# The sample's four RWKV steps on DVE, one operation at a time between the blocks' work, instead of on POOL beside it

## The chip, the cores and the metric

The kernel runs on one NeuronCore of a Trainium2 chip. The metric is the device time of one execution in microseconds (us). Before the change it is 5521.59 us, the median of three runs (5516.73 to 5526.84). The engines are TensorE (PE; PEld is its weight load), VectorE (DVE), ScalarE (ACT), GpSimd (POOL) and SyncE (SP), which here only issues DMAs.

## The reference

It is one inference step of a two-layer decoder trunk, for one prompt of 1024 tokens and for eight samples of four tokens each. The change touches layer 1's RWKV-7 mixing of the samples. Its state S has 64x64 numbers for each of 8 samples x 8 heads, and each of the four tokens takes it one step on:

```python
def step(s, inp):
    r_t, w_t, k_t, v_t, kk_t, a_t = inp
    s_kk = jnp.einsum('bhvk,bhk->bhv', s, kk_t)
    s = (s * w_t[:, :, None, :] - s_kk[..., None] * (kk_t * a_t)[:, :, None, :]
         + v_t[..., None] * k_t[:, :, None, :]).astype(s.dtype)
    return s, jnp.einsum('bhvk,bhk->bhv', s, r_t)
```

The prompt's 1024 tokens go through the same recurrence, but in a chunked form made of matrix products. Layer 1 also has a sparse attention, which needs for every query the 256 largest of its index scores; this kernel finds the 256th largest by a bitwise search.

## The kernel before

The program is a row of stages. The stage of the change is `rwkv_chunks` (L2785, tiles named `rwc_`), from 3215 to 3888 us of the span. Three pieces of work share it:

1. **The prompt's recurrence**, on PE, ACT and DVE: eight blocks of 128 tokens (the loop over `t`, numbered 0 to 7 here), each of two chunks of 64. In a block, DVE masks eight products from PSUM (`rwc_pr`, L3050), makes `rwc_NL` and `rwc_Y` (L3057 to L3061), then adds into `rwc_Y` twelve times (L3070) while PE and ACT square a triangular matrix, six rounds of two. Then come `rwc_RT` (L3076), two `rwc_ZN` (L3080), for each chunk two `rwc_Ms` and one `rwc_M` (L3089, L3094), and the block's output `rwc_y` (L3099). PE starts the next block's transposes only when `rwc_y` is done (`y_ready`), and its two steps of the state (L2995) wait for `rwc_ZN` and `rwc_M`.
2. **The search** (`key_search`, L2353; its generator `rounds`, L2386), on DVE alone. It goes over seven rows of scores (384 to 1028 wide), 32 bits, four pieces a bit, and then three pieces a row to write out the selection: 149 pieces. A piece ends at a `yield`.
3. **The sample's steps** (`rwkv_steps`, L2712, its `steps` L2750), on POOL alone: 128 partitions (sample, head, half of the values), each with 32x64 = 2048 numbers of `S` in `rwc_s_S`. A step is seven operations of 2048 elements and two sums over the keys, each sum a tree of six additions.

DVE's program sets the order by hand: `pick_round` (L3040) runs one piece of the search and stands at fixed places ("slots") of a block: after `rwc_pr` 4 and 8, after the second `rwc_Y` copy, after each of the rounds j = 1 to 5 of the `rwc_Y` additions, five more in a row behind the last of them (`for _ in range(5)`, L3073), after `rwc_RT`, after each `rwc_ZN`, after each `rwc_M`, and after `rwc_y`. That is 2+1+5+5+1+2+2+1 = 19 a block, 152 in all. What is left of the search runs behind the last block (L3102).

A `Chain` (`link`) gives each operation of the search and of the steps a semaphore that the engine itself waits for before the next one. SP issues the loads of the samples' state and vectors in block 1's place, and behind block 7 in this order: the block's `rwc_y`, seven rows of the selection (L2381), the samples' state and outputs (L2743, L2747, behind the semaphore `ready`), and the prompt's state (L2878). The next stage, `rwkv_output` (tiles `rwo_`), begins when all engines have ended this one.

Of the kernel before, what the change touches and what calls it, by code (L numbers as in the profile page):

```python
# [2 lines left out]

# [4 lines left out]
ALU = mybir.AluOpType  # L8
ACT = mybir.ActivationFunctionType
AX_X = mybir.AxisListType.X  # L10
# [768 lines left out]
def wide(ap, shape):  # L779

    return ap.broadcast_to(shape)
# [1653 lines left out]
CH = 64  # L2435

W_A, W_NB, W_K, W_R, W_V, W_LW, W_G, W_BONUS = range(8)
# [274 lines left out]
def rwkv_steps(nc, ph, A, rw, y_out, state_out):  # L2712


    VH = CH // 2
    BH = DEC_BATCH * HEADS
    S = ph.sb("s_S", [P, VH, CH])
    vec = ph.sb("s_vec", [P, DEC_SEQ, 6, CH])
    v2 = ph.sb("s_v2", [P, DEC_SEQ, VH])
    u = ph.sb("s_u", [P, VH])  # L2720
    y = ph.sb("s_y", [P, DEC_SEQ, VH])
    t1 = ph.sb("s_t1", [P, VH, CH])
    ld = ph.sem("s_ld")
    own = ph.sem("s_own")
    ready = ph.sem("s_ready")
    st = ph.sem("s_st")
    n_ld = 16 * (2 + 2 * DEC_SEQ * DEC_BATCH)

    def loads(sp):
        for x in range(2):  # L2730
            rows = slice(x * BH, (x + 1) * BH)
            sp.dma_start(S[rows, :, :].rearrange("p v k -> p (v k)"),
                         A["state_rwkv"][0].rearrange("b h (x v) k -> x (b h) (v k)", x=2)[x]).then_inc(ld, 16)
            for b in range(DEC_BATCH):
                for t in range(DEC_SEQ):
                    src = rw[SEQ + b * DEC_SEQ + t, 0:6, :].rearrange("a (h d) -> h a d", h=HEADS)
                    sp.dma_start(vec[x * BH + b * HEADS:x * BH + (b + 1) * HEADS, t, :, :], src).then_inc(ld, 16)

    def stores(sp):
        sp.wait_ge(ready, 1)  # L2740
        for x in range(2):
            rows = slice(x * BH, (x + 1) * BH)
            sp.dma_start(state_out.rearrange("b h (x v) k -> x (b h) (v k)", x=2)[x],  # L2743
                         S[rows, :, :].rearrange("p v k -> p (v k)")).then_inc(st, 16)
            for b in range(DEC_BATCH):
                dst = y_out[SEQ + b * DEC_SEQ:SEQ + (b + 1) * DEC_SEQ, :].rearrange("t (h x v) -> x h t v", h=HEADS, x=2)[x]
                sp.dma_start(dst, y[x * BH + b * HEADS:x * BH + (b + 1) * HEADS, :, :]).then_inc(st, 16)  # L2747
        sp.wait_ge(st, 16 * 2 * (1 + DEC_BATCH))

    def steps(pool):  # L2750
        link = Chain(pool, own)
        tt = nc.gpsimd.tensor_tensor
        shape = [P, VH, CH]

        def sum_keys(out):

            n = CH // 2
            while n > 1:
                link(tt(t1[:, :, 0:n], t1[:, :, 0:n], t1[:, :, n:2 * n], ALU.add))
                n //= 2  # L2760
            return tt(out.unsqueeze(2), t1[:, :, 0:1], t1[:, :, 1:2], ALU.add)

        pool.wait_ge(ld, n_ld)
        for x in range(2):
            rows = slice(x * BH, (x + 1) * BH)
            link(nc.gpsimd.tensor_copy(v2[rows, :, :], vec[rows, :, W_V, x * VH:(x + 1) * VH]))
        for t in range(DEC_SEQ):
            key = lambda a: wide(vec[:, t, a, :].unsqueeze(1), shape)
            link(tt(t1[:, :, :], S[:, :, :], key(W_A), ALU.mult))
            link(sum_keys(u[:, :]))  # L2770
            link(tt(S[:, :, :], S[:, :, :], key(W_LW), ALU.mult))
            link(tt(t1[:, :, :], wide(u[:, :].unsqueeze(2), shape), key(W_NB), ALU.mult))
            link(tt(S[:, :, :], S[:, :, :], t1[:, :, :], ALU.add))
            link(tt(t1[:, :, :], wide(v2[:, t, :].unsqueeze(2), shape), key(W_K), ALU.mult))
            link(tt(S[:, :, :], S[:, :, :], t1[:, :, :], ALU.add))
            link(tt(t1[:, :, :], S[:, :, :], key(W_R), ALU.mult))
            last = sum_keys(y[:, t, :])
            if t + 1 < DEC_SEQ:
                link(last)
        last.then_inc(ready, 1)  # L2780

    return loads, steps, stores


def rwkv_chunks(nc, A, rw, y_out, state_out, sample_state_out, scores, scores_sample, sel, sel_sample):  # L2785
# [7 lines left out]
    with Phase(nc, "rwc") as ph:  # L2793
# [50 lines left out]
        block = ph.block()  # L2844
# [5 lines left out]
        def _(sp):  # L2850
# [27 lines left out]
                sp.dma_start(state_out.rearrange("(i g) v k -> g v i k", g=2)[g], mt[:, :, g * CH:(g + 1) * CH]  # L2878
                             ).then_inc(end_st, 16)
            sp.wait_ge(end_st, 32)  # L2880

        @block.gpsimd
        def _(pool):
            sample_steps(pool)

        def sq_count(j, g):

# [147 lines left out]
        @block.vector  # L3035
        def _(dve):
            tt = nc.vector.tensor_tensor
            search = rounds(dve)

            def pick_round(dve):  # L3040
                next(search, None)

            dve.wait_ge(const_ld, n_const)
            nc.vector.memset(M[:, :, :], 0.0).then_inc(m_ready, 1)
            own = 0
            for t in range(PT):
                s = t % 2
                for h in range(HEADS):
                    dve.wait_ge(prod_mm, HEADS * t + h + 1)
                    tt(pr[:, h].rearrange("p a c -> p (a c)"), ps[:, 4 + h % 4, :],  # L3050
                       masks[:, 0:4, :].rearrange("p a c -> p (a c)"), ALU.mult).then_inc(prod_ev, 1)
                    if h % 4 == 3:
                        pick_round(dve)
                low = NL[:, 0, 1].rearrange("p (i g) c -> p g i c", g=2)
                for g in range(2):
                    dve.wait_ge(low_mm, 2 * t + g + 1)
                    tt(low[:, g], ps[:, g, :].rearrange("p (i c) -> p i c", c=P),  # L3057
                       wide(masks[:, 4, :].unsqueeze(1), [P, HP, P]), ALU.mult).then_inc(low_ev, 1)
                nc.vector.tensor_copy(Y[:, :, 0, :], x[:, s, X_A, :].rearrange("p (h d) -> p h d", h=HEADS)).then_inc(y_set, 1)
                dve.wait_ge(akv_mm, t + 1)  # L3060
                nc.vector.tensor_copy(Y[:, :, 1, :], ps[:, 2, :].rearrange("p (h d) -> p h d", h=HEADS)).then_inc(y_set, 1)  # L3061
                pick_round(dve)
                dve.wait_ge(y_set, 2 * (t + 1))
                for j in range(POW):
                    for g in range(2):
                        n = 2 * POW * t + 2 * j + g
                        dve.wait_ge(app_mm, n + 1)
                        yg = Y[:, 4 * g:4 * g + 4].rearrange("p h a c -> p (h a c)")
                        at_least(dve, app_ev, n - 1)
                        tt(yg, ps[:, 4 + g, :], yg, ALU.add).then_inc(app_ev, 1)  # L3070
                    if j:
                        pick_round(dve)
                for _ in range(5):  # L3073
                    pick_round(dve)
                dve.wait_ge(r_mm, t + 1)
                tt(RT[:, :, :], ps[:, 6, :].rearrange("p (i c) -> p i c", c=P), xT[:, :, 1, :], ALU.add).then_inc(r_ev, 1)  # L3076
                pick_round(dve)
                for c in range(2):
                    dve.wait_ge(zn_mm, 2 * t + c + 1)
                    tt(ZN[:, c, 0], ps[:, 4 + c, 0:HP * CH].rearrange("p (i k) -> p i k", k=CH),  # L3080
                       wide(eye2[:, :].unsqueeze(1), [P, HP, CH]), ALU.add).then_inc(z_ev, 1)
                    pick_round(dve)
                dve.wait_ge(pc_ev, t + 1)
                for c in range(2):
                    dve.wait_ge(step_mm, 2 * t + c + 1)
                    dve.wait_ge(zn_ev, 2 * t + c + 1)
                    for g in range(2):
                        rows = slice(64 * g, 64 * g + 64)
                        last = tt(Ms[rows, :, :], ps[rows, 2 + g, 0:HP * CH].rearrange("p (i k) -> p i k", k=CH),  # L3089
                                  ZN[rows, c, 1], ALU.add)  # L3090
                    last.then_inc(m_own, 1)
                    own += 1
                    dve.wait_ge(m_own, own)
                    tt(M[:, :, :], Ms[:, :, :], wide(pcs[:, :, c:c + 1], [P, HP, CH]), ALU.mult).then_inc(m_ready, 1)  # L3094
                    pick_round(dve)
                dve.wait_ge(y0_ev, t + 1)
                for g in range(2):
                    yv = y0[:, s, :].rearrange("p (i g v) -> p g i v", g=2, v=CH)[:, g]
                    last = tt(yv, ps[:, g, 0:HP * CH].rearrange("p (i v) -> p i v", v=CH), yv, ALU.add)  # L3099
                last.then_inc(y_ready, 1)  # L3100
                pick_round(dve)
            for _ in search:  # L3102
                pass
# [276 lines left out]
```

## Time and profile before

| | us |
|---|---|
| median of three runs | 5521.59 |
| profiled execution, its own time | 5522.32 |
| its span, first to last instruction | 5520.7 |
| DVE busy in the span | 2389.5 |
| POOL busy in the span | 979.5 |
| POOL in the samples' steps | from 3258.2 to 3427.2 |
| end of `rwc_y` of blocks 0 to 7 | 3312.2, 3419.1, 3492.9, 3568.1, 3643.1, 3717.6, 3791.8, 3867.6 |
| first instruction of the next stage on DVE | 3888.3 |

The profile is of one execution; a timeline row gives start, duration, engine, line, operation, tiles, and in brackets the idle time before it and what ended it. A row of a group gives the count behind an x, then the busy time in us, the mean of one in ns, and the idle time before. A row of windows gives the length of the stretch, then for PE, PEld, DVE, ACT and POOL the busy time and the instructions, then PE's granted clock as a share of full speed, the share of the DMA engines and their rate.

### The profile page before, as it was taken

Reading aid. Unit: us, or ns where it says so; the run is one execution under the profiler, and the core shown is the slowest. Engines: PE = TensorE matmul, PEld = TensorE weight load, DVE = VectorE, ACT = ScalarE, POOL = GpSimd, SP = SyncE. Lnnn points to the kernel's source line nnn. Section 1 sums busy time; section 2 is a strip of 40 time slices with the busy share of each in tenths; the row PEclk is TensorE's granted clock in tenths of the full one; section 3 lists DMA queues with packets and bytes.
Section 4 is the critical chain, followed back from the end, with each engine's and each line's share of the span. In section 5 each row is a group of like instructions: output and inputs, shape, how many; then the busy total and the mean of one; then the engine's idle time right before and its main releaser. Section 6 shows DMA issues by size and latency. Waiting matters only on the chain. (4 is left out here: it accounts for less than half of the span.)

```text
span 5520.7 us, 56273 instructions
## 1 busy us (share of the span) xinstructions
PE 4248.7 (77%) x21425; PEld 3301.4 (60%) x21425; DVE 2389.5 (43%) x3646; ACT 1101.7 (20%) x2150; POOL 979.5 (18%) x569
## 2 busy tenths in 40 slices
PE   7756749778799978799707866787176876999799
PEld 6534534336799956577603245677054445999667
DVE  3067640212555521210036567777596133655410
ACT  1123220110111122111014421121153201111121
POOL 2000000000122223222022338000001110222133
PEclk9855656889799989899755567878588987999899
DMA  3211010453211122222133320000413532111220
GB/s 126 72 26 23 12 30 8 134 172 88 63 46 46 38 64 70 78 98 75 51 122 104 111 77 27 28 28 3 131 37 95 159 119 76 50 46 46 64 67 31
DMA packets 239659, 377.87 MB, mean 68 GB/s; under 512 B 106923, under 2 KB 113852, under 8 KB 238079
## 3 DMA queue, kind: packets, MB, share of 16 engines
q1 hardware_dynamic: 213462, 285.77, 17.0%
q0 software_dynamic: 26000, 89.51, 5.3%
q8 instruction: 121, 1.98, 0.1%
q14 instruction: 76, 0.62, 0.0%
HBM read 292.93 MB, written 88.98 MB: 69 GB/s over the span
## 5 line engine op out<-in xcount | busy, mean ns | idle before, releaser
L91 PE MATMUL ffn_up_hp<-ffn_up_xT,ffn_up_w_high 128*128 128x352 f32 x4224 | 1017.1, 324 | 9.5 <-DVE ffn_up_xT L198 9.5
L91 PEld LDWEIGHTS ffn_up_hp<-ffn_up_xT,ffn_up_w_high 128*128 128x128 f32 x4224 | 737.5, 190 | 11.4 <-DVE ffn_up_xT L198 11.4
L91 PE MATMUL ffn_up_hp<-ffn_up_xT,ffn_up_w_low 128*128 128x352 f32 x2112 | 680.7, 322 | 0.0
L91 PEld LDWEIGHTS ffn_up_hp<-ffn_up_xT,ffn_up_w_low 128*128 128x128 f32 x2112 | 399.7, 189 | 0.0
L91 PE MATMUL ffn_down_acc<-ffn_down_w_high,ffn_down_a_high 128*128 128x512 f32 (+1 forms) x792 | 324.5, 410 | 84.3 <-DVE ffn_down_w_low L752 55.1
L91 PE MATMUL od_in_acc<-od_in_w_high,od_in_xT 128*128 128x512 f32 (+3 forms) x1152 | 353.7, 388 | 1.0 <-POOL od_in_w_low L273 1.0
L474 POOL TENSOR_TENSOR ffn_up_w_low<-ffn_up_w,ffn_up_w_high 128x1024 fp32r<-128x1024 f32 x88 | 211.3, 2401 | 760.3 <-DVE ffn_up_w_high L84 760.3
L91 PE MATMUL ffn_down_acc<-ffn_down_w_low,ffn_down_a_high 128*128 128x512 f32 (+1 forms) x792 | 319.5, 403 | 0.0
L91 PE MATMUL ffn_down_acc<-ffn_down_w_high,ffn_down_a_low 128*128 128x512 f32 (+1 forms) x792 | 318.2, 402 | 0.0
L728 POOL TENSOR_TENSOR ffn_down_a_low<-ffn_act_actT,ffn_down_a_high 128x768 fp32r<-128x768 f32 (+2 forms) x144 | 213.2, 1481 | 504.5 <-ACT ffn_down_a_high L700 504.5
L551 ACT ACTIVATE ffn_up_hb<-ffn_up_hp 128x352 f32<-128x352 f32 (+1 forms) x264 | 101.1, 456 | 884.2 <-PE ffn_up_hp L91 884.2
L91 PEld LDWEIGHTS od_in_acc<-od_in_w_high,od_in_xT 128*128 128x128 f32 (+1 forms) x1152 | 213.2, 192 | 54.1 <-POOL od_in_w_low L273 1.5
L91 PEld LDWEIGHTS ffn_down_acc<-ffn_down_w_high,ffn_down_a_high 128*128 128x128 f32 (+1 forms) x792 | 147.6, 186 | 143.5 <-issue 73.3
L767 DVE TENSOR_TENSOR ffn_down_stage<-ffn_down_acc,ffn_down_stage 128x512 f32<-128x512 f32 (+1 forms) x36 | 24.9, 691 | 464.6 <-PE ffn_down_acc L91 464.6
L2394 DVE TENSOR_SCALAR_CACHE_REDUCE rwc_work<-rwc_score,rwc_cand 128x384 f32<-128x384 f32 (+6 forms) x224 | 221.4, 988 | 4.7
L91 PE MATMUL od_in_acc<-od_in_w_low,od_in_xT 128*128 128x512 f32 (+3 forms) x576 | 222.0, 386 | 0.0
L700 ACT ACTIVATE ffn_down_a_high<-ffn_act_actT 128x768 fp32r<-128x768 f32 (+2 forms) x144 | 106.9, 744 | 445.2 <-PE ffn_down_acc L91 412.5
L84 DVE CAST ffn_up_w_high<-ffn_up_w 128x1024 fp32r<-128x1024 f32 x88 | 60.8, 693 | 298.7 <-PE ffn_up_hp L91 298.7
L576 DVE COPY ffn_up_hb<-ffn_up_cols 128x16 f32 (+1 forms) x88 | 156.7, 1780 | 74.9 <-ACT ffn_up_hb L554 74.9
L91 PE MATMUL ev_in_acc<-ev_in_w_high,ev_in_xT 128*128 128x512 f32 (+1 forms) x576 | 183.8, 398 | 1.0 <-POOL ev_in_w_low L273 1.0
L91 PEld LDWEIGHTS ffn_down_acc<-ffn_down_w_high,ffn_down_a_low 128*128 128x128 f32 (+1 forms) x792 | 147.9, 187 | 41.7 <-issue 1.5
L91 PEld LDWEIGHTS ffn_down_acc<-ffn_down_w_low,ffn_down_a_high 128*128 128x128 f32 (+1 forms) x792 | 148.1, 187 | 38.9 <-issue 1.0
(589 smaller groups left out, 7915.8 us busy)
## 6 DMA issues: line engine op xcount, KB each, us to landing
ffn_up_w<-ffn_w_in POOLq DMA_DIRECT2D x88, 512.0 KB
ffn_down_raw<-ffn_w_out SPq DMA_DIRECT2D x44, 512.0 KB, 3.9
sbs_pages<-cache_sb_k SPq DMA_DIRECT2D x64, 256.0 KB, 3.0
sbs_pages<-cache_sb_v SPq DMA_DIRECT2D x64, 256.0 KB, 2.9
rwkv_arrays<-rwi_out SPq DMA_DIRECT2D x8, 2048.0 KB, 12.6
dsas_pages<-cache_dsa_k SPq DMA_DIRECT2D x64, 256.0 KB, 3.0
dsas_pages<-cache_dsa_v SPq DMA_DIRECT2D x64, 256.0 KB, 2.9
od_in_w<-od_w_in POOLq DMA_DIRECT2D x7, 2048.0 KB, 10.9
```

Source lines behind the costliest of these rows:

```text
L84: return nc.vector.tensor_copy(out, x)
L91: last = nc.tensor.matmul(out, a[p], b[q], start=start and i == 0, stop=stop and i == 2)
L474: nc.gpsimd.tensor_tensor(w_low[:, q], w[:, q], w_high[:, q], ALU.subtract).then_inc(low_done[q], 1)
L551: nc.scalar.activation(hb[:, q, 2 + b * THIRD:2 + c1], hp[:, q, b, 0:c1 - b * THIRD], ACT.Copy).then_inc(ev_done[q], 1)
L576: nc.vector.tensor_copy(kept[:, :, 0:2], cols[:, f, 0:2 * DEC_BATCH] .rearrange("p (b r) -> p b r", r=2)).then_inc(dve_own, 1)
L700: nc.scalar.activation(unit_part(a_high, n, u), act_unit(n, u), ACT.Copy).then_inc(a_high_done, 1)
L728: nc.gpsimd.tensor_tensor(unit_part(a_low, n, u), act_unit(n, u), unit_part(a_high, n, u), ALU.subtract).then_inc(a_low_done, 1)
L767: nc.vector.tensor_tensor(x, acc[0:r, n % NB, :], x, ALU.add).then_inc(ev_done, 1)
L2394: link(ts(scratch(i, i % 2), row(i), of(cand, i), 0.0, op, ALU.add, accum_out=of(count, i)))
```

## The change

`steps` becomes a generator for DVE that yields after every operation. The two trees of additions become one `tensor_reduce` each, so a step has nine operations, and four steps 36. The generator is chained behind the search, POOL's program for the stage is gone, and the row of five slots becomes one of nine, so a block has 23 slots and the stage 184. The arithmetic is the same but for the order of the sums. In the changed kernel the line numbers are one higher ahead of the steps, three higher in SP's program of the stage, and one lower in DVE's (`rwc_RT` is L3075).

```diff
-    def steps(pool):
-        link = Chain(pool, own)
-        tt = nc.gpsimd.tensor_tensor
+    def steps(dve):
+        link = Chain(dve, own)
+        tt = nc.vector.tensor_tensor
         shape = [P, VH, CH]
-        def sum_keys(out):
-            n = CH // 2
-            while n > 1:
-                link(tt(t1[:, :, 0:n], t1[:, :, 0:n], t1[:, :, n:2 * n], ALU.add))
-                n //= 2
-            return tt(out.unsqueeze(2), t1[:, :, 0:1], t1[:, :, 1:2], ALU.add)
-        pool.wait_ge(ld, n_ld)
+        dve.wait_ge(ld, n_ld)
...
-            link(nc.gpsimd.tensor_copy(v2[rows, :, :], vec[rows, :, W_V, x * VH:(x + 1) * VH]))
+            link(nc.vector.tensor_copy(v2[rows, :, :], vec[rows, :, W_V, x * VH:(x + 1) * VH]))
         for t in range(DEC_SEQ):
             key = lambda a: wide(vec[:, t, a, :].unsqueeze(1), shape)
             link(tt(t1[:, :, :], S[:, :, :], key(W_A), ALU.mult))
-            link(sum_keys(u[:, :]))
+            yield
+            link(nc.vector.tensor_reduce(u[:, :], t1[:, :, :], AX_X, ALU.add))
+            yield
             link(tt(S[:, :, :], S[:, :, :], key(W_LW), ALU.mult))
+            yield
...
             link(tt(t1[:, :, :], S[:, :, :], key(W_R), ALU.mult))
-            last = sum_keys(y[:, t, :])
+            yield
+            last = nc.vector.tensor_reduce(y[:, t, :], t1[:, :, :], AX_X, ALU.add)
             if t + 1 < DEC_SEQ:
                 link(last)
-        last.then_inc(ready, 1)
+            else:
+                last.then_inc(ready, 1)
+            yield
...
-        @block.gpsimd
-        def _(pool):
-            sample_steps(pool)
...
-            search = rounds(dve)
+            search = itertools.chain(rounds(dve), sample_steps(dve))
...
-                for _ in range(5):
+                for _ in range(9):
                     pick_round(dve)
```

DVE in block 6, around `rwc_RT`, before. `rwc_work`, `rwc_score`, `rwc_count` and `rwc_cand` are the search's tiles:

```order
L2394 TENSOR_SCALAR rwc_work,rwc_count<-rwc_score,rwc_cand 128x896
L2394 TENSOR_SCALAR rwc_work,rwc_count<-rwc_score,rwc_cand 128x1024
L3076 TENSOR_TENSOR rwc_RT<-rwc_ps,rwc_xT 128x512
L2394 TENSOR_SCALAR rwc_work,rwc_count<-rwc_score,rwc_cand 32x1028
L2405 TENSOR_SCALAR rwc_short<-rwc_count 128x7
L2412 TENSOR_SCALAR rwc_flip<-rwc_short 128x7
L2413 TENSOR_TENSOR rwc_cand<-rwc_cand,rwc_flip 128x7
L3080 TENSOR_TENSOR rwc_ZN<-rwc_ps,rwc_eye 128x256
```

and now, at the same place (`rwc_s_` are the tiles of the samples' steps, `rwc_s_t` is the scratch `t1`):

```order
L2426 TENSOR_TENSOR rwc_work<-rwc_work 32x1028
L2427 TENSOR_SCALAR rwc_score<-rwc_work 32x1028
L2759 COPY rwc_s_v<-rwc_s_vec 64x128 x2
L2762 TENSOR_TENSOR rwc_s_t<-rwc_s_S,rwc_s_vec 128x2048
L2764 TENSOR_REDUCE rwc_s_u<-rwc_s_t 128x32
L2766 TENSOR_TENSOR rwc_s_S<-rwc_s_S,rwc_s_vec 128x2048
L2768 TENSOR_TENSOR rwc_s_t<-rwc_s_u,rwc_s_vec 128x2048
L2770 TENSOR_TENSOR rwc_s_S<-rwc_s_S,rwc_s_t 128x2048
L2772 TENSOR_TENSOR rwc_s_t<-rwc_s_v,rwc_s_vec 128x2048
L3075 TENSOR_TENSOR rwc_RT<-rwc_ps,rwc_xT 128x512
L2774 TENSOR_TENSOR rwc_s_S<-rwc_s_S,rwc_s_t 128x2048
L3079 TENSOR_TENSOR rwc_ZN<-rwc_ps,rwc_eye 128x256
```

Before, the search is still at its last bit here; now it ends here, and the first six operations of the steps stand between it and `rwc_RT`, the next ones behind `rwc_RT` and `rwc_ZN`.

DVE at the end of block 7, from the second `rwc_ZN` on, before:

```order
L3080 TENSOR_TENSOR rwc_ZN<-rwc_ps,rwc_eye 128x256
L2425 TENSOR_TENSOR rwc_work<-rwc_work 32x1028
L2426 TENSOR_SCALAR rwc_score<-rwc_work 32x1028
L3089 TENSOR_TENSOR rwc_Ms<-rwc_ps,rwc_ZN 64x256 x2
L3094 TENSOR_TENSOR rwc_M<-rwc_Ms,rwc_pcs 128x256
L3089 TENSOR_TENSOR rwc_Ms<-rwc_ps,rwc_ZN 64x256 x2
L3094 TENSOR_TENSOR rwc_M<-rwc_Ms,rwc_pcs 128x256
L3099 TENSOR_TENSOR rwc_y<-rwc_ps,rwc_y 128x4x64 x2
```

and now:

```order
L3079 TENSOR_TENSOR rwc_ZN<-rwc_ps,rwc_eye 128x256
L2770 TENSOR_TENSOR rwc_s_S<-rwc_s_S,rwc_s_t 128x2048
L3088 TENSOR_TENSOR rwc_Ms<-rwc_ps,rwc_ZN 64x256 x2
L3093 TENSOR_TENSOR rwc_M<-rwc_Ms,rwc_pcs 128x256
L2772 TENSOR_TENSOR rwc_s_t<-rwc_s_v,rwc_s_vec 128x2048
L3088 TENSOR_TENSOR rwc_Ms<-rwc_ps,rwc_ZN 64x256 x2
L3093 TENSOR_TENSOR rwc_M<-rwc_Ms,rwc_pcs 128x256
L2774 TENSOR_TENSOR rwc_s_S<-rwc_s_S,rwc_s_t 128x2048
L3098 TENSOR_TENSOR rwc_y<-rwc_ps,rwc_y 128x4x64 x2
L2776 TENSOR_TENSOR rwc_s_t<-rwc_s_S,rwc_s_vec 128x2048
L2778 TENSOR_REDUCE rwc_s_y<-rwc_s_t 128x32
```

Before, the slots behind both `rwc_M` and behind `rwc_y` are empty, because the search has run out; now each holds an operation of 2048 elements, and the last sum follows behind the last block.

## Rows read from the trace of the kernel before

**Rows 1.** The page, first part: busy time, share of the span, instructions.

```profile
PE 4248.7 (77%) x21425; PEld 3301.4 (60%) x21425; DVE 2389.5 (43%) x3646; ACT 1101.7 (20%) x2150; POOL 979.5 (18%) x569
```

**Rows 2.** Windows of blocks 0, 1, 2-7: length, busy PE PEld DVE ACT POOL, clock.

```profile
3229.80:3312.30 82.50, 56.13 (x512) 54.23 (x509) 65.77 (x114) 12.29 (x22) 51.92 (x29) 0.72 0.19 41
3312.30:3419.10 106.80, 57.52 (x536) 54.93 (x536) 91.50 (x117) 14.68 (x26) 103.43 (x44) 0.71 0.06 18
3419.10:3867.60 448.50, 340.08 (x3216) 326.35 (x3216) 326.51 (x653) 88.04 (x156) 7.62 (x7) 0.79 0.07 22
```

**Rows 3.** Timeline of POOL: the steps' first multiply and last sum (start, us).

```profile
3258.92 4.55 POOL L2769 TENSOR_TENSOR rwc_s_t<-rwc_s_S,rwc_s_vec 128x2048 f32<-128x2048 f32 x1
...
3426.95 0.24 POOL L2761 TENSOR_TENSOR rwc_s_y<-rwc_s_t 128x32 f32<-128x32 f32 x1
```

**Rows 4.** Groups of DVE lines while POOL runs its steps (3217 to 3428).

```profile
L2410 DVE TENSOR_TENSOR rwc_cand<-rwc_cand,rwc_flip 128x7 int32<-128x7 int32 x8 | 21.8, 2721 | 0.3
...
L3094 DVE TENSOR_TENSOR rwc_M<-rwc_Ms,rwc_pcs 128x256 f32<-128x256 f32 x4 | 13.0, 3250 | 0.1
```

**Rows 5.** The same DVE groups once POOL is quiet (3428 to 3868).

```profile
L3094 DVE TENSOR_TENSOR rwc_M<-rwc_Ms,rwc_pcs 128x256 f32<-128x256 f32 x12 | 5.1, 425 | 0.4
...
L2410 DVE TENSOR_TENSOR rwc_cand<-rwc_cand,rwc_flip 128x7 int32<-128x7 int32 x22 | 3.7, 167 | 0.8
```

**Rows 6.** Timeline of DVE around block 6: one bit of the search, then landmarks.

```profile
3695.57 0.61 DVE L2394 TENSOR_SCALAR_CACHE_REDUCE rwc_work<-rwc_score,rwc_cand 128x384 f32<-128x384 f32 x1
...
3703.43 0.69 DVE L3076 TENSOR_TENSOR rwc_RT<-rwc_ps,rwc_xT 128x512 f32<-128x512 f32 x1
...
3716.84 0.76 DVE L3099 TENSOR_TENSOR rwc_y<-rwc_ps,rwc_y 128x256 f32<-128x256 f32 x2
...
3723.55 2.48 DVE L3050 TENSOR_TENSOR rwc_pr<-rwc_ps,rwc_masks 128x512 f32<-128x512 f32 x4 [4.11 <-PE rwc_ps L2922]
...
3765.12 1.29 DVE L3070 TENSOR_TENSOR rwc_Y<-rwc_ps,rwc_Y 128x512 f32<-128x512 f32 x2
...
3781.19 0.42 DVE L3080 TENSOR_TENSOR rwc_ZN<-rwc_ps,rwc_eye 128x256 f32<-128x256 f32 x1
...
3791.01 0.76 DVE L3099 TENSOR_TENSOR rwc_y<-rwc_ps,rwc_y 128x256 f32<-128x256 f32 x2
```

**Rows 7.** Waits within block 6: us in total, times, longest.

```profile
PE rwc_ps L2995 <- ACT rwc_ZN L3007: 7.1, 1, 7.1
```

**Rows 8.** Groups of DVE by shape: a reduce and a tensor_tensor with long rows.

```profile
L2075 DVE TENSOR_REDUCE qkn_stat<-qkn_sq 128x16 f32<-128x1024 f32 x8 | 9.7, 1218 | 10.5 <-ACT qkn_sq L2062 10.4
...
L814 DVE TENSOR_TENSOR s_in_flat<-s_R,s_in_F 128x2048 f32<-128x2048 f32 x1 | 2.3, 2293 | 0.0
```

**Rows 9.** Groups by shape, 3420 to 3860: one tensor_scalar of 1024.

```profile
L2426 DVE TENSOR_SCALAR rwc_score<-rwc_work 128x1024 f32<-128x1024 f32 x1 | 0.7, 694 | 0.0
```

**Rows 10.** Groups by shape, whole span: one scalar_tensor_tensor of 1024.

```profile
L190 DVE SCALAR_TENSOR_TENSOR od_in_norm_rows<-od_in_norm_rows,od_in_stat 128x1024 f32<-128x1024 f32 x8 | 13.2, 1656 | 0.3
```

**Rows 11.** Timeline of DVE at the end of block 7.

```profile
3860.18 1.21 DVE L2425 TENSOR_TENSOR rwc_work<-rwc_work 32x1028 f32<-32x1028 f32 x1
3861.42 0.68 DVE L2426 TENSOR_SCALAR rwc_score<-rwc_work 32x1028 f32<-32x1028 f32 x1
...
3865.51 0.86 DVE L3089 TENSOR_TENSOR rwc_Ms<-rwc_ps,rwc_ZN 64x256 f32<-64x256 f32 x2 [2.16 <-PE rwc_ps L2996]
...
3866.86 0.76 DVE L3099 TENSOR_TENSOR rwc_y<-rwc_ps,rwc_y 128x256 f32<-128x256 f32 x2
```

**Rows 12.** Timeline of SyncE's queue behind block 7.

```profile
3868.00 3.69 SPq L2381 DMA_DIRECT2D selected<-rwc_score  x6
...
3872.88 1.18 SPq L2743 DMA_DIRECT2D out_rwkv_sample<-rwc_s_S  x1
```

**Rows 13.** Windows: the end of block 1, the next block's squarings.

```profile
3376.60:3419.10 42.50, 8.00 (x141) 7.49 (x137) 41.60 (x51) 0.95 (x3) 41.01 (x20) 0.50 0.00 0
3434.80:3450.80 16.00, 15.14 (x117) 15.14 (x118) 6.21 (x13) 5.67 (x10) 0.00 (x0) 0.84 0.00 1
```

More of the change, by code:

```diff
@@ L1 @@
+import itertools
 import math
@@ L2769, in steps @@
             link(tt(t1[:, :, :], S[:, :, :], key(W_A), ALU.mult))
-            link(sum_keys(u[:, :]))
+            yield
+            link(nc.vector.tensor_reduce(u[:, :], t1[:, :, :], AX_X, ALU.add))
+            yield
             link(tt(S[:, :, :], S[:, :, :], key(W_LW), ALU.mult))
+            yield
             link(tt(t1[:, :, :], wide(u[:, :].unsqueeze(2), shape), key(W_NB), ALU.mult))
+            yield
             link(tt(S[:, :, :], S[:, :, :], t1[:, :, :], ALU.add))
+            yield
             link(tt(t1[:, :, :], wide(v2[:, t, :].unsqueeze(2), shape), key(W_K), ALU.mult))
+            yield
             link(tt(S[:, :, :], S[:, :, :], t1[:, :, :], ALU.add))
+            yield
             link(tt(t1[:, :, :], S[:, :, :], key(W_R), ALU.mult))
-            last = sum_keys(y[:, t, :])
+            yield
+            last = nc.vector.tensor_reduce(y[:, t, :], t1[:, :, :], AX_X, ALU.add)
             if t + 1 < DEC_SEQ:
                 link(last)
-        last.then_inc(ready, 1)
+            else:
+                last.then_inc(ready, 1)
+            yield
     return loads, steps, stores
```

## The prediction

> **What bounds the kernel now.** I read the page first: PE is busy 77% of the span, DVE 43%, POOL 18% [rows 1]. That says nothing of the stage in which the change lies, so next came the windows of that stage, cut at the ends of `rwc_y`. Blocks 2 to 7 take 448.5 us together, 74.75 each; block 1 takes 106.8, and block 0, which starts here with its first `rwc_pr`, 82.5 [rows 2]. Then POOL's timeline: the steps run from 3258.9 to 3427.2, which is nearly all of block 1 and two thirds of block 0 [rows 3]. So the two long blocks are those in which POOL works. The groups of DVE say why: while POOL runs, the search's seven-element `rwc_cand` takes 2721 ns on the mean and `rwc_M` 3250; afterwards 167 and 425 [rows 4, 5]. Single operations of DVE stand still behind POOL's long ones, such as that of 4.55 us [rows 3].
>
> Within a clean block the timeline of block 6 shows two regimes. From the first `rwc_pr` (3723.55) to the last additions of the twelve (ending 3765.12 + 1.29) DVE and PE hand work to each other; behind that DVE runs without a gap through the search's pieces to `rwc_ZN` at 3781.19 and on to `rwc_y` [rows 6], while PE, done with its products, waits 7.1 us for the `rwc_ZN` that stands behind them [rows 7]. So the tail of every block is bound by DVE: an operation put into the row of slots lengthens the block by its own duration.
>
> **What the change takes away.** POOL's steps are off the path themselves: they end at 3427.2, and SP asks for their result at 3872.88, behind the last block [rows 3, 12]. What they cost is what they do to DVE. Block 1 is longer than a clean one by 106.8 - 74.75 = 32.05 us. Block 0 lacks the wait ahead of the first `rwc_pr`, which in block 6 is 3723.55 - (3716.84 + 0.76) = 5.95; a clean block without it takes 68.8, so block 0 is longer by 13.7 [rows 2, 6]. Sum 45.8 us, all of which goes, since POOL has no instruction left in the stage. Two lines alone carry 8 x (2721 - 167) + 4 x (3250 - 425) = 31.7 us of it [rows 4, 5], and both lie in DVE's own run.
>
> **What it adds.** 36 operations of 2048 elements: 28 `tensor_tensor` and 8 `tensor_reduce`. The trace has a `tensor_tensor` of 128x2048 between SBUF tiles with 2293 ns, and a `tensor_reduce` of 1024 with 1218, from which I estimate 2.28 for 2048, twice 1218 less one start-up [rows 8]. Each is linked to the next; between two linked operations the timeline shows 3861.42 - (3860.18 + 1.21) = 0.03 us [rows 11]. 36 x 2.32 = 83.5, and 0.6 for the two copies of `v2`: 84.1 us. POOL's version, with its trees, held more operations, but none of that was on the path.
>
> The step operations have forms (an operand broadcast along the keys or the values) that DVE shows only at other sizes, so I bound them. From below: a one-source `tensor_scalar` of 1024 takes 694 ns, doubled 1.39 [rows 9]. From above: a `scalar_tensor_tensor` of 1024 takes 1656, doubled 3.3 [rows 10]. I take the row of the same operation and size.
>
> **What hides some of it.** The four new slots a block do not add work of their own; they draw the search forward. A bit of it takes 3703.43 - 3695.57 = 7.86 us in four pieces, 1.97 each [rows 6], so every block grows by that, the search ends 12 slots ahead of block 6's end (149 pieces in 6 x 23 + 11 slots), and 34 of the step operations fill the slots from there to the last `rwc_y`. It is therefore simplest to count DVE's work: 84.1 us more, less what falls where nobody waits for DVE:
> - Behind the last `rwc_y` come one multiply and the last sum, 2 x 2.32 = 4.6 us. SP meanwhile issues the selection's rows from 3868.00 until 3872.88, which is 5.25 us behind the end of `rwc_y` (3866.86 + 0.76), and only then needs the steps' result [rows 11, 12]. Hidden, with half a microsecond to spare; the sum ends 4.65 behind `rwc_y`.
> - In block 7 the slot behind the first `rwc_M` was empty and DVE waited there 2.16 us for PE's step [rows 11]: 2.2 hidden.
> - Some five slots of block 7 lie under waits for PE (behind `rwc_pr` 8, the second copy, and the rounds 1 to 3); there an operation of 2.32 takes the place of a piece of 1.97: 5 x 0.35 = 1.7 hidden.
>
> Sum hidden 8.5. On the path 84.1 - 8.5 = 75.6. Net +75.6 - 45.8 = +29.8 us.
>
> No queue is crossed: SP's loads of the samples still stand in block 1's place, some 450 us ahead of their new use, POOL issued no DMA here, and the wait on `ld` that moves to DVE has long been met when DVE reaches it. Behind the stage nothing changes.
>
> The profiled execution took 5522.3 us (span 5520.7 and 1.6 around it), the median 5521.6. So 5522.3 + 29.8 = 5552.1 by the profiled run; against the median 5551.4. I say **5551**.
>
> **Rivals.**
>
> *Cover (not slower).* PE, not DVE, could bound the row of slots, and then the added operations are free. This decides block by block: with 45.8 gained, every microsecond of cover per block takes off 8, and 3.7 us per block bring the net to zero; if all 32 new slots were covered, 63 us go and the time is 5522 + 30 - 63 = 5489. For it: DVE does wait for PE inside the rounds. Against it: PE already waits 7.1 us for DVE at the end of the row [rows 7], so the cover is used up before the first new slot. Chance 0.06, half of it faster and half no change.
>
> *Cheap operations.* If the steps ran at the doubled 1.39 us, 36 x 1.42 + 0.6 = 51.7, less some 6 hidden, less 45.8: the time stays at about 5522. For it only the rate of the one-source form; against it two rows of the very operations. Chance 0.03, no change.
>
> *The faster engine wins.* POOL's operation of 2048 takes 4.55 us, DVE's 2.29 [rows 3, 8]; if the steps' own 168 us (3258.9 to 3427.2) were on the path, the change would bring 168 - 84 and more, some 5440 us. Against it: their result lies 445 us before it is fetched. Chance 0.01. The Trainium skill, page "GPSIMD Engine Reference", section "4.1 Engine selection", advises VectorE for elementwise work, at about half the time; by that rule this change is a gain. The trace bears out the ratio, but not the conclusion: POOL's time was spent beside the path, and DVE's is spent on it.
>
> *A colder PE (slower still).* PE's idle time in a block's tail grows from 7 to 15 us. If the rounds then began at the lower level, their first 16 us, with a granted clock of 0.84 and PE busy 15.1, would come at 0.50 and cost 15.1 x (0.84/0.50 - 1) = 10 us a block, 80 in all: 5632. Against it: block 2's rounds showed that 0.84 right behind a stretch of 42.5 us at 0.50 (1.2 GHz) with PE busy 8.0 [rows 13], and block 2 was no longer than the other clean ones. A longer rest costs nothing that a short one doesn't. Chance 0.04. The Trainium skill, page "TensorE: Matmul & The Clock Gate", section "Part 1: The HAM clock gate", has idle time bring the engine back to 1.2 GHz; by it the blocks' beginnings would be slower, but the tails lie at the low level already.
>
> **How the numbers follow.** The forecast has 0.86, cover 0.06, cheap operations 0.03, the faster engine 0.01, the colder PE 0.04. A measurement of this kernel can tell about 0.2%, 11 us, from no change: faster 0.03 + 0.01 = 0.04, no change 0.03 + 0.03 = 0.06 and 0.01 from the low end of the forecast, slower 0.89. The forecast's own spread: the operations may take 2.2 to 2.5 us each (-4, +7), the hidden part may be 3 to 20 us (+5, -12), and what POOL's end gives back 38 to 50 (+8, -4), so about -16 and +17. The range of 5534 to 5570 holds that and little of the rivals.
>
> **What would show it.** In the changed kernel's profile: `rwc_cand` at 167 ns and `rwc_M` at 425 throughout; block 0 near 68.8 + 7.9 = 77 us from its first `rwc_pr`, blocks 1 to 4 near 82.6 each, blocks 6 and 7 near 90; step operations of 2.28 to 2.30 us; PE's wait ahead of L2995 (there L2994 or so) near 15 us a block; SP not waiting for the steps behind the selection's rows. It is wrong if blocks 1 to 4 are near 75 (the row was covered), if the steps' operations are far from 2.3, if the rounds' pitch changes, or if block 1 stays long without POOL.

## The result and the profile after

The changed kernel takes 5547.3 us, median of 5 runs (5546.9 to 5549.8); before on the same chip 5521.6. The ratio is 1.0047, with a 95% interval of 1.0035 to 1.0058: **25.7 us slower**, forecast 29.8. Run once more beside later experiments it stood 27.2 us above before (1.0042, 1.0025 to 1.0059).

The page's busy line of the profile after answers to [rows 1]:

```profile
PE 4255.5 (77%) x21425; PEld 3314.6 (60%) x21425; DVE 2424.0 (44%) x3684; ACT 1101.2 (20%) x2150; POOL 816.8 (15%) x491
```

POOL has lost its 163 us of steps, DVE has 34.5 more. Now the windows of block 0, blocks 1 to 4 together, and blocks 5, 6 and 7, for [rows 2]:

```profile
3231.40:3308.40 77.00, 56.15 (x512) 54.26 (x509) 59.88 (x131) 12.29 (x22) 0.00 (x0) 0.73 0.21 45
3308.40:3636.00 327.60, 229.94 (x2144) 220.86 (x2144) 248.57 (x533) 58.73 (x104) 0.00 (x0) 0.76 0.07 23
3636.00:3713.70 77.70, 60.45 (x536) 58.12 (x536) 58.84 (x119) 14.68 (x26) 0.00 (x0) 0.74 0.07 25
3713.70:3803.70 90.00, 61.54 (x536) 59.05 (x536) 72.74 (x82) 14.68 (x26) 0.00 (x0) 0.71 0.07 21
3803.70:3890.70 87.00, 54.99 (x536) 52.84 (x536) 71.58 (x60) 14.62 (x26) 0.00 (x0) 0.76 0.01 4
```

The two blocks that POOL had stretched are short again (block 1: 81.2 instead of 106.8), and all the others are longer. From the first `rwc_pr` to the end of the last `rwc_y` it is 659.3 us instead of 637.8: +21.5. The stage's start is 1.6 us later and what follows it 1.5 longer, in all 24.6 between the two profiles.

The groups of DVE in the stage show both sides of the trade, for [rows 4, 5, 8]:

```profile
L2762 DVE TENSOR_TENSOR rwc_s_t<-rwc_s_S,rwc_s_vec 128x2048 f32<-128x2048 f32 x4 | 9.1, 2287 | 0.1
...
L2764 DVE TENSOR_REDUCE rwc_s_u<-rwc_s_t 128x32 f32<-128x2048 f32 x4 | 9.1, 2281 | 0.1
...
L3093 DVE TENSOR_TENSOR rwc_M<-rwc_Ms,rwc_pcs 128x256 f32<-128x256 f32 x16 | 6.8, 425 | 0.6
...
L2411 DVE TENSOR_TENSOR rwc_cand<-rwc_cand,rwc_flip 128x7 int32<-128x7 int32 x30 | 5.0, 166 | 1.0
```

`rwc_M` and `rwc_cand` run at their free durations in every block; the new operations take 2.28 to 2.29 us, whatever their broadcast. The timeline of DVE at the end of block 7, for [rows 11]:

```profile
3872.31 2.29 DVE L2764 TENSOR_REDUCE rwc_s_u<-rwc_s_t 128x32 f32<-128x2048 f32 x1
3874.64 0.69 DVE L3075 TENSOR_TENSOR rwc_RT<-rwc_ps,rwc_xT 128x512 f32<-128x512 f32 x1
3875.24 2.28 DVE L2766 TENSOR_TENSOR rwc_s_S<-rwc_s_S,rwc_s_vec 128x2048 f32<-128x2048 f32 x1
3877.56 0.42 DVE L3079 TENSOR_TENSOR rwc_ZN<-rwc_ps,rwc_eye 128x256 f32<-128x256 f32 x1
...
3889.98 0.76 DVE L3098 TENSOR_TENSOR rwc_y<-rwc_ps,rwc_y 128x256 f32<-128x256 f32 x2
3890.65 2.28 DVE L2776 TENSOR_TENSOR rwc_s_t<-rwc_s_S,rwc_s_vec 128x2048 f32<-128x2048 f32 x1
3892.97 2.29 DVE L2778 TENSOR_REDUCE rwc_s_y<-rwc_s_t 128x32 f32<-128x2048 f32 x1
```

and SyncE's queue behind it, for [rows 12]:

```profile
3890.76 0.32 SPq L2861 DMA_DIRECT2D rwkv_y<-rwc_y  x1
...
3896.01 1.19 SPq L2744 DMA_DIRECT2D out_rwkv_sample<-rwc_s_S  x1
```

No row shows an idle time: DVE runs from step to step with the block's own work between them, so an operation of 2.3 us ahead of `rwc_y` lengthens the block as long as PE's own work there is shorter (e3 shows where that ends). The last sum ends at 3895.26, 0.75 ahead of the store that needs it.

### The profile page after: what moved, and what is told of

Its sections match the earlier page's. It is cut to its first block and busy times, and to the rows that moved or that the text cites. A ratio compares the mean times of both kernels' runs of the same rounds, so it can differ in the third digit from the quotient of the medians.

```text
span 5545.3 us, 56234 instructions
## 1 busy us (share of the span) xinstructions
PE 4255.5 (77%) x21425; PEld 3314.6 (60%) x21425; DVE 2424.0 (44%) x3684; ACT 1101.2 (20%) x2150; POOL 816.8 (15%) x491
## 5 line engine op out<-in xcount | busy, mean ns | idle before, releaser
L92 PEld LDWEIGHTS ffn_up_hp<-ffn_up_xT,ffn_up_w_high 128*128 128x128 f32 x4224 | 737.6, 190 | 11.4 <-DVE ffn_up_xT L199 11.4
```

The lines of the kernel that those rows point to most:

```text
L92: last = nc.tensor.matmul(out, a[p], b[q], start=start and i == 0, stop=stop and i == 2)
```

## The experiments

Lines of a kernel derived from the one before are those of before up to the steps; where the steps are cut out, later lines are 13 lower. "Stage" is the time from the first `rwc_pr` to the end of the last `rwc_y`, by the profile.

**e1, the steps left out.** What does POOL's work cost DVE? In the kernel before, POOL's four steps are not computed; one memset of their output and the semaphore remain.

```diff
-        for t in range(DEC_SEQ):
...
-        last.then_inc(ready, 1)
+        nc.gpsimd.memset(y[:, :, :], 0.0).then_inc(ready, 1)
```

> The kernel before with POOL's four steps left out (the samples' states go out as loaded, their outputs as zeros); the loads, the stores and the five slots stay. Theory (POOL's operations held single operations of DVE, and that was on the path for 45.8 us): 5522 - 46 = 5476 us, blocks 0 and 1 as long as blocks 2 to 7 (about 69 and 75 us), rwc_cand at 167 ns throughout. Rival (blocks 0 and 1 are long because of the loads that SP issues there, or for being the first): 5522 us, blocks 0 and 1 still 82 and 107 us.

Measured: 5475.5 against 5516.4, ratio 0.9925 (0.9909 to 0.9942), -40.9 us. Its groups of DVE in the stretch of [rows 4]:

```profile
L3081 DVE TENSOR_TENSOR rwc_M<-rwc_Ms,rwc_pcs 128x256 f32<-128x256 f32 x4 | 1.7, 425 | 0.1
...
L2410 DVE TENSOR_TENSOR rwc_cand<-rwc_cand,rwc_flip 128x7 int32<-128x7 int32 x10 | 1.7, 167 | 0.3
```

and its windows of block 0, block 1 and blocks 2 to 7, which stand against [rows 2]:

```profile
3230.82:3300.08 69.26, 55.58 (x512) 53.84 (x509) 52.43 (x114) 12.29 (x22) 0.78 (x3) 0.76 0.22 49
3300.08:3374.22 74.14, 60.87 (x536) 58.54 (x536) 54.59 (x117) 14.68 (x26) 0.00 (x0) 0.75 0.08 26
3374.22:3824.48 450.26, 344.56 (x3216) 330.52 (x3216) 326.56 (x653) 88.03 (x156) 0.00 (x0) 0.78 0.07 22
```

Blocks 0 and 1 shrink by 13.2 and 32.7, the other six stay within 2 us: the stage is 593.7, 44.2 below before. DVE's busy time falls from 2389.5 to 2338.6 us, 50.9 less with the same instructions, so POOL's cost lay in what it did to DVE; below this is called POOL's lock. The run also gives the other price: the changed kernel's stage less this one's is **65.7 us** for the same steps on DVE.

**e2, five slots.** The changed kernel with its row left at five, so that the search keeps its old places and most of the steps come behind the last block.

```diff
-                for _ in range(9):
+                for _ in range(5):
```

> The changed kernel with five slots in the row instead of nine; everything is still computed. The search then ends three slots ahead of the end of block 7, and 33 of the 36 operations follow behind the last block, where SP waits for them. Theory (the row's slots are bound by DVE, so it costs the same to run the operations in them or behind): blocks 1 to 6 near 75 us, 33 x 2.32 = 77 us behind the last block of which SP's stores hide 5; some 5551 us, 0 to 8 us above the changed kernel. Rival (PE's work covers the row, the operations in it are free): the changed kernel hides 32 pieces and this one none, 60 us slower, 5610.

Measured: 5557.7, ratio 1.0073 (1.0056 to 1.0089), +41.3, against +27.2 for the changed kernel. Blocks 1 to 6 take 74.2 to 75.4, as in e1. SyncE's queue behind them:

```profile
3835.09 1.09 SPq L2382 DMA_DIRECT2D selected_sample<-rwc_score  x1
3909.90 0.52 SPq L2744 DMA_DIRECT2D out_rwkv_sample<-rwc_s_S  x1
```

SyncE is done with the selection at 3836.18 and waits 73.7 us for the samples; DVE runs 33 operations there in a row, until 3909.88. So the added slots are not what costs; the operations are, and behind the block next to nothing covers them (5.2 us of SyncE's). From the first `rwc_pr` to the samples' store it is 675.6 against 664.6 in the changed kernel, +11.0. I had expected 0 to 8 more, and missed it because the changed kernel hides more than I counted (18.4 us instead of 8.5, see below).

**e3, two steps.** The changed kernel with tokens 2 and 3 of each sample not computed: 18 operations less.

```diff
-        for t in range(DEC_SEQ):
+        link(nc.vector.memset(y[:, 2:DEC_SEQ, :], 0.0))
+        for t in range(2):
```

> The changed kernel with two of the four steps (tokens 2 and 3 of the samples left out, their outputs zero): 18 operations fewer, 41.8 us of DVE. Theory (an operation costs its 2.32 us where PE waits for DVE and nothing where it doesn't): the 17 slots emptied in block 7 are one in the rounds that is free, one that is half free, eleven around the row of which PE's own 7 us must be left in, four behind rwc_ZN and rwc_M of which about half counts, and the two last behind rwc_y, free; 25 to 28 us saved, 5520 us. Rival (each operation costs its full time wherever it stands): 5505. Rival (the added time is something else, such as PE's clock): nothing moves in proportion, 5535 or more.

Measured: 5522.3, ratio 1.0011 (1.0002 to 1.0021), +5.9 on before, 20 to 21 less than the changed kernel. The stage is 639.2, 20.2 less, and block 7 holds all of it: 66.8 instead of 87.0. DVE in block 7, from the last addition of the rounds on:

```profile
3846.42 0.69 DVE L3070 TENSOR_TENSOR rwc_Y<-rwc_ps,rwc_Y 128x512 f32<-128x512 f32 x1 [0.20 <-PE rwc_ps L2956]
3848.30 0.69 DVE L3076 TENSOR_TENSOR rwc_RT<-rwc_ps,rwc_xT 128x512 f32<-128x512 f32 x1 [1.20 <-PE rwc_ps L2963]
3855.87 0.42 DVE L3080 TENSOR_TENSOR rwc_ZN<-rwc_ps,rwc_eye 128x256 f32<-128x256 f32 x1 [6.88 <-PE rwc_ps L2983]
3858.34 0.42 DVE L3080 TENSOR_TENSOR rwc_ZN<-rwc_ps,rwc_eye 128x256 f32<-128x256 f32 x1 [2.04 <-PE rwc_ps L2983]
3859.77 0.86 DVE L3089 TENSOR_TENSOR rwc_Ms<-rwc_ps,rwc_ZN 64x256 f32<-64x256 f32 x2 [1.00 <-PE rwc_ps L2996]
...
3863.25 0.86 DVE L3089 TENSOR_TENSOR rwc_Ms<-rwc_ps,rwc_ZN 64x256 f32<-64x256 f32 x2 [2.16 <-PE rwc_ps L2996]
```

The 16 operations ahead of `rwc_y` that went are 16 x 2.32 = 37.1 us of DVE; 20.2 came back, and DVE now waits for PE's products instead: 1.20 + 6.88 + 2.04, and 1.00 + 2.16 ahead of the `rwc_Ms`, 13.3 together. Neither "all of it" nor my 25 to 28 holds: once the row is empty, PE bounds the tail.

**e4, the slots in the waits.** e3's rows show waits inside the rounds, too. The changed kernel with all steps, but seven of the row's slots moved to places where DVE waits for PE: behind both additions of rounds 0 to 3 and one of 4 and 5, a second one behind the second `rwc_Y` copy, and a second one behind `rwc_y`. It stays at 23 a block.

```diff
+                pick_round(dve)
...
-                    if j:
-                        pick_round(dve)
-                for _ in range(9):
+                        if g or j < 4:
+                            pick_round(dve)
+                for _ in range(2):
...
+                pick_round(dve)
```

> The changed kernel, all computed, 23 slots a block as before, but seven of the row's nine moved to where DVE waits for PE: five in the rounds (behind the first addition of j = 0 to 3 and the second of j = 0), a second one behind rwc_y and a second one behind the last copy into rwc_Y. Theory (a slot costs only where PE waits for DVE; a wait in the rounds is 1.8 to 2.0 us, about one piece of 1.97): the row shrinks by 7 x 1.97 = 13.8 us a block, the rounds grow by 1 to 3 us, in all 85 to 100 us less than the changed kernel, about 5455. Rival (the additions of the rounds are on PE's path too, so a piece between them costs its time there): 5547, no change.

Measured: **5450.0** (5446.1 to 5454.0) against 5516.4, ratio 0.9881 (0.9864 to 0.9897): 66.4 us faster than before and some 92 faster than the changed kernel, by their distances from before, with the same work on the same engine. That is within the 85 to 100 expected. The stage is 572.3. The rounds of blocks 0 to 5 are no longer than with one slot each (25.6 to 26.6 us; 25.5 to 26.6 there), and the row shrinks from 17.6 to 20.1 us to 3.7 to 6.3. The blocks are of two kinds, though: 0, 1, 4 and 5 take 62 to 69 us, 2 and 3 take 75 (6 and 7, which hold the steps, 80.5 and 75.8). DVE's timeline at `rwc_ZN` of blocks 1 and 2:

```profile
3343.75 0.42 DVE L3080 TENSOR_TENSOR rwc_ZN<-rwc_ps,rwc_eye 128x256 f32<-128x256 f32 x1
...
3418.27 0.43 DVE L3080 TENSOR_TENSOR rwc_ZN<-rwc_ps,rwc_eye 128x256 f32<-128x256 f32 x1 [5.41 <-PE rwc_ps L2982]
```

and the windows of PE's products behind the last addition in the same two blocks:

```profile
3335.40:3344.90 9.50, 9.46 (x155) 9.16 (x156) 9.11 (x22) 1.16 (x3) 0.00 (x0) 0.91 0.01 2
3404.60:3420.30 15.70, 15.70 (x155) 15.35 (x158) 9.90 (x23) 1.16 (x3) 0.00 (x0) 0.50 0.00 1
```

The same 155 matmuls take 9.5 us in the one and 15.7 in the other, at a granted clock of 0.91 (most of it at the upper level, 2.4 GHz) and of 0.50 (1.2 GHz). With the row nearly empty, PE's level decides the tail.

**e5, the slots in the waits and the steps on POOL.** Does the move pay by itself, then? The kernel before with its five slots moved into the rounds in e4's way.

```diff
-                    if j:
-                        pick_round(dve)
-                for _ in range(5):
+                        if g or j < 4:
+                            pick_round(dve)
+                for _ in range(0):
```

> The steps stay on POOL as before; the five slots of the row move into the rounds j = 0 to 3, which then have a slot behind each of their two additions. The question is whether the steps on DVE pay once the search sits in DVE's waits. Theory (the place of a slot and POOL's lock are two costs that add up): row and wait for the products, 14.4 us in a clean block, fall to about 8.5 where PE's products run at their faster level and to 13.5 where they don't, six blocks of the one kind and two of the other: about -37 us, and the lock of about 44 stays; so 37 us below the kernel before, about 5480 (5465 to 5500), and e4 with the steps on DVE stays about 30 ahead. Rival one: POOL's lock falls into waits once the row is empty and costs little; then about 75 below before, 5445, and POOL is the better place. Rival two: PE is slow in every block's tail and the row was covered; then within 15 us of before.

Measured: 5499.1 against 5521.3 on that chip, ratio 0.9955 (0.9939 to 0.9972), -22.2 where 37 were expected. Windows of block 0, block 1 and the rest:

```profile
3236.13:3324.27 88.14, 57.61 (x512) 55.59 (x509) 71.49 (x114) 12.29 (x22) 58.24 (x30) 0.73 0.18 40
3324.27:3429.18 104.91, 65.79 (x536) 63.13 (x536) 88.59 (x118) 14.69 (x26) 101.54 (x44) 0.70 0.06 18
3429.18:3856.30 427.12, 345.69 (x3216) 332.08 (x3216) 323.50 (x653) 88.11 (x156) 3.09 (x6) 0.80 0.07 23
```

Blocks 2 to 7 gain 21.4 us and block 1 gains 1.9; block 0 loses 5.6. The profiled execution took 5513.6 us, 14.5 above the median, so its stage, 620.2, may be some us long. Its groups of DVE while POOL runs:

```profile
L2410 DVE TENSOR_TENSOR rwc_cand<-rwc_cand,rwc_flip 128x7 int32<-128x7 int32 x8 | 26.3, 3285 | 0.3
L3070 DVE TENSOR_TENSOR rwc_Y<-rwc_ps,rwc_Y 128x512 f32<-128x512 f32 x24 | 16.2, 689 | 8.5 <-PE rwc_ps L2956 7.1 <-DVE rwc_work L2394 0.7
L3094 DVE TENSOR_TENSOR rwc_M<-rwc_Ms,rwc_pcs 128x256 f32<-128x256 f32 x4 | 8.6, 2153 | 0.1
```

The locked `rwc_cand` now stands between two additions that PE waits for: the rounds of blocks 0 and 1 take 36.6 and 39.4 us instead of some 26. Rival one of this run is refuted: the lock doesn't hide in the waits.

**e6, the slots in the waits and no steps.** e5 with POOL's steps left out as in e1.

> As e5, and the samples' steps are left out altogether (their output is not computed). It gives the price of the steps on either engine with the slots in the rounds. Theory: 44 us below e5 (the lock's price, as in e1 against before), so about 5436 (5420 to 5455), and e4, which does the steps on DVE, is then only some 14 us above it against 66 in the row. Rival: within 15 us of e5, since the lock hides in the waits.

Measured: 5450.5, ratio 0.9868 (0.9852 to 0.9885), -70.8; 48.6 below e5, as the theory had it (44), and e4 within 5 us of it. From `rwc_RT` to `rwc_ZN`, blocks 1 and 3, each window behind that of the row:

```profile
3341.55:3343.38 1.83, 1.78 (x18) 1.45 (x19) 1.69 (x6) 0.00 (x0) 0.00 (x0) 0.68 0.00 0
3343.38:3354.79 11.41, 11.41 (x99) 11.39 (x100) 1.97 (x6) 0.67 (x2) 0.00 (x0) 0.50 0.00 0
3490.91:3492.80 1.89, 1.83 (x23) 1.66 (x24) 1.82 (x6) 0.00 (x0) 0.00 (x0) 1.00 0.00 0
3492.80:3498.44 5.64, 5.64 (x96) 5.62 (x97) 3.04 (x6) 0.67 (x2) 0.00 (x0) 1.00 0.01 3
```

Blocks 0, 3, 4 and 7 are like block 3 (7.5 us from the last addition to `rwc_ZN`), blocks 1, 2, 5 and 6 like block 1 (13.1 to 13.2). I had guessed six to two; two more blocks at the lower level are 2 x 5.6 = 11 us of the 14.5 that e6 lacks against its expectation. In e5 five blocks are at the lower level there (13.0 to 13.8 us) and only 3, 4 and 7 at the upper (7.5): three more than guessed, 17 us, about the 14.8 that e5 lacks.

**The changed kernel again**, on the chip of e5 and e6.

> The changed kernel once more, so that it stands on the chip of the experiments. Theory: 26 us above before, as measured at first (20 to 31), which leaves e2 15 us above it and so five slots with the rest of the steps behind the stage worse than nine. Rival: the first chip differs, and here it stands with e2, about 41 above before.

Measured: 5548.5 against 5521.3, ratio 1.0042 (1.0025 to 1.0059), +27.2. With the first measurement's +25.7 it stands some 26 above before on both occasions, so e2's +41.3 is put down to e2 itself; e1 to e4 ran on another chip, on which the changed kernel was not run.

Together, difference to before on the same chip by the runs, and the stage by the profile, in us:

| the steps | slots in a row | slots in the rounds |
|---|---|---|
| on POOL | 0; 637.8 | -22.2; 620.2 (e5) |
| on DVE | +25.7; 659.3 | -66.4; 572.3 (e4) |
| left out | -40.9; 593.7 (e1) | -70.8; 566.4 (e6) |

By the stage, POOL's lock costs 44 in the row and 54 in the rounds; by the runs it is 41 and 49, with some 10 us either way, so the runs do not show that it costs more in the rounds. What stood still is the same: DVE is busy 50.9 us longer in before than in e1, and 50.3 longer in e5 (2389.4) than in e6 (2339.1). In the row some 7 of that were hidden, in the rounds none; and some 6 of the 10 us between 44 and 54 are PE's products in block 0, which ran at 0.50 in e5 and at 1.00 in e6 (13.8 and 7.5 us from the last addition to `rwc_ZN`). The steps on DVE cost 66 in the row and 6 in the rounds. e4 has 23 slots a block and e6 has 19, so the 6 is not the steps' price alone.

## Why the prediction was right, and which term was off

The direction, the mechanism and the time (5551 for 5547) held. Point by point:

- **The lock goes**: forecast 45.8, by e1 44.2. The two lines are free throughout, and block 0 is 77.0 (forecast 77).
- **The operations cost what a `tensor_tensor` of that size cost**: 36 of 2.27 to 2.29 us, 2.32 from start to start, as taken from [rows 8]. The two far bounds were not needed. The rival of cheap operations is refuted.
- **The row is not covered**: blocks 1 to 4 take 81.2 to 82.4 (forecast 82.6), and the row is longer by one bit of the search, 7.86, in each. Blocks 6 and 7 take 89.9 and 87.0 (forecast near 90). The cover rival is refuted, but my evidence was thinner than I wrote. I read PE's wait in block 6 alone, 7.1 us [rows 7]; in block 5 of the same kernel the trace has

```profile
PE rwc_ps L2995 <- ACT rwc_ZN L3007: 0.3, 1, 0.3
```

  and in block 4 none. PE's products run at the lower level there (granted clock 0.54 in block 5 and 0.52 in block 4), and they end just as the old row ends. In e1, where POOL is quiet, blocks 0 and 1 show no such wait either. So in half of the blocks the forecast held without a margin: had PE's products been a microsecond longer there, about a microsecond of the new slots would have been covered. That they were no longer is luck; my argument saw only a block that had 7.1 to spare. After the change, PE's wait in blocks 2 and 4:

```profile
PE rwc_ps L2994 <- ACT rwc_ZN L3006: 14.9, 1, 14.9
...
PE rwc_ps L2994 <- ACT rwc_ZN L3006: 6.8, 1, 6.8
```

  The forecast of "near 15 us a block" holds in blocks 2, 3, 6 and 7 (12.0 to 16.7) and fails in 0, 1, 4 and 5 (6.0 to 7.8). The windows of the row in blocks 2 and 4 say why, 8.76 us of PE against 15.84:

```profile
3437.17:3457.29 20.12, 8.76 (x152) 8.43 (x152) 19.28 (x43) 0.78 (x2) 0.00 (x0) 0.78 0.00 1
...
3601.70:3620.70 19.00, 15.84 (x152) 15.31 (x152) 18.09 (x44) 0.77 (x2) 0.00 (x0) 0.51 0.00 1
```

- **What hides some of it**: this is the term that was mis-sized, 8.5 forecast. Against e1 84.1 us were added and 65.7 are on the path, so 18.4 hid. By stretches of the blocks, summed over all eight, e1 to after: ahead of the first `rwc_pr` -3.7, masks +1.8, from `rwc_NL` to the first addition -2.3, rounds +1.6, row +64.9, `rwc_RT` to `rwc_y` +3.5. 4.6 us lie behind `rwc_y`, as forecast, and SyncE did not wait for the steps. Under waits for PE in the rounds and in the tail lie 3.4 and 4.3 (DVE's busy time grew by 5.0 and 7.7 there, the stretches by 1.6 and 3.5), against a forecast of 1.7 and 2.2. And 6.0 is what no term foresaw: two stretches became shorter. PE's transposes ahead of `rwc_pr`, block 3, after:

```profile
3471.56:3476.79 5.23, 4.98 (x27) 4.58 (x29) 1.28 (x4) 2.39 (x4) 0.00 (x0) 0.60 0.78 239
```

  and in e1:

```profile
3449.45:3455.27 5.82, 5.57 (x27) 4.99 (x29) 1.28 (x5) 2.39 (x4) 0.00 (x0) 0.54 0.79 241
```

  The same 27 matmuls take 0.59 us less, which is the stretch's whole difference, at a granted clock of 0.60 instead of 0.54. The rival of a colder PE had the wrong sign: PE had rested longer ahead of this stretch, and more of the stretch lay at its upper level. Whether the one made the other is open, and so is the cause of the -2.3. The rounds, which that rival would have slowed, ran at a granted clock of 0.98 to 1.00 in every block of before and of the changed kernel. The row that I set against it [rows 13] does not begin right behind the stretch at 0.50 but 15.7 us later, and takes in some 6 us ahead of the first addition. And the tails, which I had at the low level already, were there only from `rwc_RT` on (0.50 in every block of before); the products ahead of that ran at 1.00 in blocks 2, 3, 6 and 7.
- **The sum**: 65.7 - 44.2 = 21.5 in the stage instead of 75.6 - 45.8 = 29.8. Some 3 us outside the stage, for which I had no term, brought the total nearer to the forecast than its parts were. That is luck: the program ahead of the stage is the same in all nine profiles, and the stage begins anywhere from 3225.2 to 3236.1. The interval of the runs, 1.0035 to 1.0058, is 19 to 32 us, so the total alone could not have shown that the term was off.
- **The faster engine wins**: this rival did not come, as forecast. The ratio of the two engines, 4.55 to 2.29 us, is the one that the Trainium skill states (page "GPSIMD Engine Reference", section "4.1 Engine selection"), and still the change lost: POOL's 168 us lay beside the path, DVE's 65.7 on it. Only with DVE's waits as their place (e4) does the Trainium skill's choice win.

## What to carry to other kernels

Here work that fills in on an engine cost its full duration where that engine bounds, and little where it waits: e4 did what the changed kernel does and was 92 us faster, by the place of seven slots. Before moving work off a slow helper engine, price two things apart, what the helper does to its neighbour (leave its work out once) and what the new place costs there. And read a cover in every repetition of a loop: block 6 had 7.1 us of it, block 5 had 0.3.

## What the runs showed of the hardware that I had not expected

- **Two levels in one loop.** PE's products at the end of a block ran at a granted clock near 1.00 (2.4 GHz) in some blocks and at 0.50 (1.2 GHz) in others (e6: 5.6 to 6.2 us against 10.6 to 11.4 from `rwc_RT` to `rwc_ZN`). Just before them PE had waited for the last addition: 1.60, 1.12, 1.60 and 3.32 us in the blocks that stayed at the upper level, 2.49, 1.95, 2.49 and 1.96 in those that fell. The 3.32 of block 7 keeps this from being a rule by the last wait alone; what decides is open. The row of slots had hidden this in the kernel before.
- **A lock on one-source operations as well.** In e5's timeline a seven-element `tensor_scalar` of 0.17 us, too, stood still until POOL's operation ended:

```profile
3264.49 4.52 POOL L2769 TENSOR_TENSOR rwc_s_t<-rwc_s_S,rwc_s_vec 128x2048 f32<-128x2048 f32 x1
...
3265.50 3.54 DVE L2405 TENSOR_SCALAR rwc_short<-rwc_count 128x7 int32<-128x7 f32 x1
3269.08 0.17 DVE L2409 TENSOR_SCALAR rwc_flip<-rwc_short 128x7 int32<-128x7 int32 x1
```

  (L2405 takes 2644 ns there on the mean of nine, and 171 in before once POOL is quiet), while the additions into `rwc_Y`, with one source in PSUM, kept their 689 ns. The Trainium skill, page "SBUF — State Buffer", section "Who interferes with whom", names both: a DVE operation with two sources in SBUF meets POOL's reads, and a `tensor_scalar` can meet them in one of its modes. The rows agree, down to the addition that is spared.
